# A hybrid decoder trunk on one core: first two projection units of layer 2 computed from g times the residual sum

## The reference, cut to what matters

```python
z = x @ w_in[l]            # -> q | k | v | conv h, B, C | mem q | gate_a | gate_c | gate_m
...
x = layer_norm(ALPHA * x + mix, ln1_g[l], ln1_b[l])
x = layer_norm(ALPHA * x + ffn(x), ln2_g[l], ln2_b[l])
```

## Time and profile before

| | |
|---|---|
| median of 3 runs | 1547.05 us (1546.71 to 1547.48) |
| profiled execution | 1547.15 us, span of its core 1545.4 us |
| mean granted TensorE clock | 0.996 of full speed |
| TensorE busy | 1523.5 us, 99% of the span |
| VectorE / ScalarE / GpSimd busy | 1124.1 / 928.3 / 144.8 us |
| DMA | 416.62 MB, mean 270 GB/s |

### The profile page before, as it was taken

The page is one execution under the profiler, slowest core; times in us unless marked ns, Lnnn a source line. Parts: engine busy times, 40 slices in busy tenths (PEclk is TensorE's granted clock), DMA queues, the critical chain, the costliest instruction groups (busy, mean ns, idle before and its releaser), DMA issues.

```text
span 1545.4 us, 22921 instructions
## 1 busy us (share of the span) xinstructions
PE 1523.5 (99%) x9077; PEld 1349.0 (87%) x9077; DVE 1124.1 (73%) x1043; ACT 928.3 (60%) x974; POOL 144.8 (9%) x182
## 2 busy tenths in 40 slices
PE   8999999999999999999999999999999999999997
PEld 7999999999999899999688888888888888888786
DVE  5547658844443636567798888888888888889997
ACT  5444445633333654444677777777777777767775
POOL 3203003300002103002230000000000000020000
PEclk9999999999999999999999999999999999999999
DMA  9845634694444345432799999999999999999981
GB/s 311 276 140 173 174 112 142 241 378 145 148 140 154 122 150 161 134 110 82 269 392 389 395 390 357 384 383 390 369 351 382 386 387 362 361 389 377 392 322 61
DMA packets 226425, 416.62 MB, mean 270 GB/s; under 512 B 8592, under 2 KB 110368, under 8 KB 224752
## 3 DMA queue, kind: packets, MB, share of 16 engines
q1 hardware_dynamic: 217712, 383.28, 70.4%
q0 software_dynamic: 8608, 31.89, 5.7%
HBM read 393.99 MB, written 23.11 MB: 270 GB/s over the span
## 4 chain that ended last, share of the span: by engine, by line
PE 96%; DVE 2%; ACT 1%; DMA 0%; issue 0%; POOL 0%; SPq 0%; DVEq 0%; POOLq 0%; ACTq 0%
PE ps L1950 13%; PE ps L1952 13%; PE ps L1951 13%; PE ps L2485 11%; PE ps L2487 11%; PE ps L2486 11%; PE ps L2467 5%; PE ps L2469 5%; PE ps L2468 5%; PE ps L2496 1%; PE ps L2046 1%; PE ps L2017 1%; PE ps L1985 0%; PE ps L1986 0%; PE ps L1987 0%; PE ps L2074 0%
## 5 line engine op out<-in xcount | busy, mean ns | idle before, releaser
L1338 DVE TENSOR_TENSOR low<-raw,high 128x2048 fp32r<-128x2048 f32 x264 | 603.7, 2291 | 88.0 <-ACT high L948 86.7
L948 ACT ACTIVATE high<-raw 128x2048 fp32r<-128x2048 f32 x264 | 505.9, 1919 | 197.3 <-PE ps L2487 125.1
L1348 DVE TENSOR_TENSOR low<-raw,high 128x2048 fp32r<-128x2048 f32 (+1 forms) x91 | 206.7, 2274 | 196.9 <-ACT high L941 196.8
L1950 PE MATMUL ps<-xh,high 128*128 128x320 f32 x1056 | 332.1, 315 | 4.3 <-DVE xl L1561 2.7
L1951 PE MATMUL ps<-xh,low 128*128 128x320 f32 x1056 | 327.6, 310 | 0.0
L1952 PE MATMUL ps<-xl,high 128*128 128x320 f32 x1056 | 327.6, 310 | 0.0
L2485 PE MATMUL ps<-high,xeh 128*128 128x512 f32 (+1 forms) x768 | 291.5, 380 | 0.0
L2487 PE MATMUL ps<-high,xel 128*128 128x512 f32 (+1 forms) x768 | 288.8, 376 | 0.0
L2486 PE MATMUL ps<-low,xeh 128*128 128x512 f32 (+1 forms) x768 | 287.6, 374 | 0.0
L941 ACT ACTIVATE high<-raw 128x2048 fp32r<-128x2048 f32 (+1 forms) x91 | 172.2, 1892 | 144.1 <-PE ps L1952 120.4
L1950 PEld LDWEIGHTS ps<-xh,high 128*128 128x128 f32 x1056 | 199.8, 189 | 10.8 <-issue 9.4
(11 more groups left out here) (398 smaller groups left out, 1671.9 us busy)
## 6 DMA issues: line engine op xcount, KB each, us to landing
raw<-in_exp_w_gate_dram SPq DMA_DIRECT2D x88, 1024.0 KB, 7.7
raw<-in_exp_w_up_dram SPq DMA_DIRECT2D x88, 1024.0 KB, 7.6
raw<-in_exp_w_down_dram SPq DMA_DIRECT2D x88, 1024.0 KB, 7.5
raw<-in_w_in_dram SPq DMA_DIRECT2D x37, 1024.0 KB, 5.3
ybuf<-zeros POOLq DMA_DIRECT2D x12, 1024.0 KB, 19.8
raw<-in_ffn_w_gate_dram SPq DMA_DIRECT2D x11, 1024.0 KB, 5.3
raw<-in_ffn_w_up_dram SPq DMA_DIRECT2D x11, 1024.0 KB, 6.7
raw<-in_w_o_dram SPq DMA_DIRECT2D x8, 1024.0 KB, 5.1
```

What stands on the lines that cost most here:

```text
L948: act.activation(high[(N_DENSE + m) % HI_RING][:, :], raw_moe[s][:, :], ACT.Copy).then_inc(hi_done, 1)
L1338: dve.tensor_tensor(low_moe[s][:, :], raw_moe[s][:, :], high[(N_DENSE + m) % HI_RING][:, :].bitcast(F32), ALU.subtract).then_inc(lo_done, 1)
L1348: dve.tensor_tensor(low[n % RING][:, cols], raw[n % RING][:, cols], high[n % HI_RING][:, cols].bitcast(F32), ALU.subtract).then_inc(lo_don ...
L1950: pe.matmul(out, wh, ah, start=first, stop=False)
```

## The change

The method of the first norm is brought to the second. v = g * r is split while the down projection runs, the units z 0 and z 1 of layer 2 run on v, and their four output tiles are corrected by mean and scale on VectorE (`first_projections`) into a new SBUF tile zfix; ScalarE takes the tiles from there and adds the column of b with its bias. Other than at the first norm, unit z 0 is done with all its k ahead of unit z 1, and its two corrections stand between the normalised tiles 5 and 6. v lies where kstage and the memory tiles lie, so the loads of layer 2's first keys and values go behind unit z 1. z tile 4 goes to bank 6, and the first key transposes wait for its copy. Unit z 2 is the first to read xh and xl, with a wait for each k. The two matmuls for nothing go. The waits for the blank of `ybuf` go to the third of the twelve units of the down projection.

```diff
--- before.py
+++ after.py
@@ -360,9 +362,12 @@
...
+        v_at = (mix_at + 8 * KD * T, kstage_at)
+        vh = [at(f"vh{i}", [P, KD, TV], F32R, v_at[i]) for i in range(2)]
+        vl = [at(f"vl{i}", [P, KD, TV], F32R, v_at[i] + 4 * KD * TV) for i in range(2)]
+        V_VEC = (0, 32)
+        rscale = [stats[i][:, S1, :] for i in range(2)]
+        zfix = at("zfix", [P, 4, T], F32, mix_at + 4 * KD * T)
@@ -439,7 +444,7 @@
...
+        MEAN = (ps[:, BUSY, FOLD:FOLD + T], ps[:, BUSY, FOLD:FOLD + T], ps[:, 3, 0:T])
@@ -604,7 +610,9 @@
...
-            turn = l * (len(OUTS) - len(MEM_BORROWS)) + q - (len(MEM_BORROWS) if q >= MEM_LAST[0] else 0)
+            if (l, q) == (1, 4):
+                return 6
+            turn = l * (len(OUTS) - len(MEM_BORROWS) + (q > 4)) + q - (len(MEM_BORROWS) if q >= MEM_LAST[0] else 0)
             return 3 if (l, q) == (1, 3) else turn % 3
@@ -852,6 +860,10 @@
...
+                if l == 1:
+                    pool.wait_ge(unit_done, UNIT_OF[("z", 1, 1)] + 1)
+                    load_mem_k(1, 0)
+                    load_mem_v(1, 0)
@@ -871,11 +883,6 @@
...
-                if l == 0:
-                    pool.wait_ge(tr_mm, e0 + EVENT_NO[("wink", 0, 0)] + 1)
-                    load_mem_k(1, 0)
-                    pool.wait_ge(pv_mm, j0 + 4)
-                    load_mem_v(1, 0)
@@ -1036,16 +1043,26 @@
...
-                wait_out(act, l, ("z", f))
-                src = ps[:, out_bank(l, OUT_NO[("z", f)]), 0:T]
+                if l == 1 and f < 4:
+                    act.wait_ge(zfixed, f + 1)
+                    src, bias = zfix[:, f, :], fix[:, f, 1:2]
+                else:
+                    wait_out(act, l, ("z", f))
+                    src, bias = ps[:, out_bank(l, OUT_NO[("z", f)]), 0:T], None
+                def taken(out, of, columns):
+                    if bias is None:
+                        return act.activation(out, columns, ACT.Copy)
+                    return act.activation(out, columns, ACT.Identity, bias=bias[of, :])
@@ -1096,19 +1115,19 @@
...
-                if L == 0:
-                    v_high(KD - 2)
+                if split:
+                    v_high(L, KD - 2)
                 square(L, KD - 1)
-                if L == 0:
-                    v_high(KD - 1)
+                if split:
+                    v_high(L, KD - 1)
                 act.wait_ge(var_done, L + 1)
                 act.activation(fold_dev, fold_dev, ACT.Sqrt, bias=eps[:, 0:1]).then_inc(std_done, 1)
                 act.wait_ge(mean_mm, L + 1)
                 act.activation(stats[L % 2][:, MU, :], MEAN[L], ACT.Copy).then_inc(mean_cp, 1)
-                if L == 0:
-                    hi(UNIT_OF[("fg", 0, 0)] + AHEAD)
-                    act.wait_ge(rstd_mm, 1)
-                    act.activation(by_fold(rscale), rstd, ACT.Copy, scale=float(D)).then_inc(rscale_done, 1)
+                if split:
+                    hi(UNIT_OF[("fg", 0, 0) if L == 0 else ("z", 1, 0)] + AHEAD)
+                    act.wait_ge(rstd_mm, L + 1)
+                    act.activation(by_fold(rscale[L]), rstd, ACT.Copy, scale=float(D)).then_inc(rscale_done, 1)
@@ -1120,6 +1139,9 @@
...
+                    if L == 1 and f == 5:
+                        for q in range(2):
+                            z_copy(1, q)
@@ -1127,8 +1149,11 @@
...
-                    hi(n + AHEAD)
-                    if u[0] == "z":
+                    if l == 1 and i == 0:
+                        hi(n + 1 + AHEAD)
+                    elif l == 0 or i > 1:
+                        hi(n + AHEAD)
+                    if u[0] == "z" and not (l == 1 and i == 0):
@@ -1198,7 +1223,11 @@
...
-            act.wait_ge(y_blank, 16 * ROUNDS * NE // 2)
+                    if i == 3:
+                        act.wait_ge(y_blank, 16 * ROUNDS * NE // 2)
+                        v_columns(1)
+                    v_high(1, 2 * (i // 3) - 2)
+                    v_high(1, 2 * (i // 3) - 1)
@@ -1516,19 +1545,29 @@
...
+            def first_projections(f):
+                t = zfix[:, f, :]
+                bank = out_bank(1, OUT_NO[("z", f)])
+                wait_out(dve, 1, ("z", f))
+                link(dve.tensor_copy(fix[:, f, :], ps[:, bank, T:TV]))
+                link(dve.scalar_tensor_tensor(t, stats[1][:, MU, :], fix[:, f, 0:1], ps[:, bank, 0:T], ALU.mult, ALU.add))
+                dve.tensor_tensor(t, t, rscale[1], ALU.mult).then_inc(zfixed, 1)
@@ -1568,12 +1607,15 @@
...
-                    if f == 2 and L == 0:
-                        v_low(KD - 1)
+                    if f == 2:
+                        v_low(L, KD - 1)
                     if f >= 4:
                         low_part(f - 2)
-                    if f == 5 and L == 0:
-                        lo(UNIT_OF[("fg", 0, 0)] + AHEAD)
+                    if f == 5 and L == 1:
+                        for q in range(2):
+                            first_projections(q)
+                    if f == 5:
+                        lo(UNIT_OF[("fg", 0, 0) if L == 0 else ("z", 1, 0)] + AHEAD)
@@ -1588,6 +1630,14 @@
...
+                    if l == 1 and i < 2:
+                        if i == 1:
+                            for f in (2, 3):
+                                first_projections(f)
+                            scores(l, 0)
+                            pending = 0
+                            lo(UNIT_OF[u] + AHEAD)
+                        continue
@@ -1696,9 +1746,16 @@
...
+                if i == 4:
+                    v_low_columns(1)
+                if p >= 1 and part == 1:
+                    v_low(1, 2 * p - 2)
+                    v_low(1, 2 * p - 1)
...
+                    if p == 3:
+                        v_low(1, KD - 2)
@@ -2006,6 +2063,8 @@
...
+                if l == 1 and e == EVENTS[0]:
+                    pe.wait_ge(z_cp, 38 + 5)
@@ -2134,10 +2193,13 @@
...
+                if l == 1 and q == 4:
+                    pe.wait_ge(rscale_done, 2)
+                    return
@@ -2188,8 +2250,8 @@
...
+                if L < 2:
+                    pe.wait_ge(mean_cp, L + 1)
@@ -2199,17 +2261,30 @@
...
-                for k in range(KD):
-                    pe.wait_ge(xl_done, KD + k + 1)
-                    for q in range(4):
...
-                        last = product(ps[:, out_bank(1, q), 0:T], wh[:, c], wl[:, c], xh[:, k, :], xl[:, k, :],
-                                       k == 0, k == KD - 1)
...
+                def projection(k, q):
+                    wh, wl = parts[q // 2]
+                    c = slice(256 * k + 128 * (q % 2), 256 * k + 128 * (q % 2) + 128)
+                    return product(ps[:, out_bank(1, q), 0:TV], wh[:, c], wl[:, c], vh[1][:, k, :], vl[1][:, k, :],
+                                   k == 0, k == KD - 1)
+                pe.wait_ge(resid, KD + KD - 2)
+                pe.wait_ge(v_lo, KD + 1 + 2)
+                projection(0, 1)
+                projection(0, 2)
+                last_sums(1)
+                projection(0, 0)
+                projection(0, 3)
+                for unit in range(2):
+                    for k in range(1, KD):
+                        if unit == 0:
+                            pe.wait_ge(v_lo, KD + 1 + k + 2)
+                        for m in range(2):
+                            last = projection(k, 2 * unit + m)
+                            if (unit, k, m) == (0, 1, 1):
+                                spread(1)
+                            if k == KD - 1:
+                                last.then_inc(unit_done if m else out_mm, 1)
@@ -2260,6 +2335,8 @@
...
+                            if l == 1 and i == 2 and m == 0:
+                                pe.wait_ge(xl_done, KD + k + 1)
@@ -2348,7 +2425,6 @@
...
-            layer_norm(1)
```

More of the change, by code:

```diff
@@ L330, in build_trunk @@
         kvtok = take("kvtok", [P, 2, 3, P])
+        kstage_at = place["at"]
         kstage = take("kstage", [P, 4, 2, 256])
@@ L1046, in z_copy @@
                         to, of = slice(64 * kv, 64 * kv + 64), slice(64 * a, 64 * a + 64)
-                        act.activation(qT[to, g, :], src[of, 0:NP], ACT.Copy)
-                        last = act.activation(qS[to, :, g, :], src[of, NP:T].rearrange("p (b t) -> p b t", t=TS), ACT.Copy)
+                        taken(qT[to, g, :], of, src[of, 0:NP])
+                        last = taken(qS[to, :, g, :], of, src[of, NP:T].rearrange("p (b t) -> p b t", t=TS))
                 elif 6 <= f < 8:
@@ L1055, in z_copy @@
                     act.wait_ge(zeroed, 2 * l + 2)
-                    act.activation(qmT[:, p, :], src[:, 0:NP], ACT.Copy)
+                    taken(qmT[:, p, :], slice(0, P), src[:, 0:NP])
                     for a in range(2):
                         h = slice(64 * a, 64 * a + 64)
-                        last = act.activation(qm_diag[h, p, :, (2 * p + a) * 8:(2 * p + a) * 8 + 8],
-                                              src[h, NP:T].rearrange("p (b t) -> p b t", t=8), ACT.Copy)
```

(34 more changed lines are left out.)

41 lines of the change are left out of this document (18 added, 23 removed).

## The result

| | before | after |
|---|---|---|
| median of 13 runs each, same chip | 1546.63 us (1545.4 to 1547.48) | 1550.12 us (1548.67 to 1551.26) |
| profiled execution; span | 1547.15 us; 1545.4 | 1550.54 us; 1548.8 |

The ratio of after to before is 1.0022, with a 95% interval of 1.0015 to 1.0029. So the change costs 3.4 us (2.3 to 4.5). Forecast were +1.8 us and 1548.9; the time lies inside the range, at its slow side.

What follows compares the result with a forecast made beforehand. TensorE, busy 99% of the span, was taken to bound the kernel. A paper gain of 4.4 us lost to a 4.7 us wait left +0.3; with +1.5 for the clock, +1.8 on 1547.15 gave 1548.9 us, range 1545.0 to 1550.9.

Steps and rivals of the forecast that it cites:

- TensorE up to the scores: Second norm into layer 2: sums at 506.21, scores at 524.8 instead of 528.10, 4.4 us won on paper by 532.1.
- The new pause: TensorE in z 0, before the product of k 7: 1.6 us waiting for the low half of v tile 7.
- The point of comparison: Start of layer 2's cached-key transposes on TensorE, taken as 536.46 in the kernel before.
- VectorE: Corrections of z 0 and z 1 at 1.18 us each, the last ending at 529.54; maxima of the scores to 531.0.
- ScalarE, the mis-sized term: Last corrected tile taken at 529.6 in 1.01 us; behind the Exp load, z tile 4 copied at 536.7.
- The added wait: TensorE before the key transposes waits 4.7 us for z tile 4's copy: +0.3 against 536.46.
- The key load: Layer 2's keys, issued at 523.8, land 530.0 to 533.0 under the wait; without it, up to 0.9 us.
- The clock, the second mis-sized term: Behind the long pause before the key transposes, one 1.2 GHz stretch: +1.5 us, bounds 0 and 3.0.
- Rival 3: Fourth unit: two low-clock stretches and a late z tile 4 copy, 0.3 + 3.0 + 0.5 = +3.8, 1550.9; chance 0.15.
- Rival 1: Long pause before the key transposes swallows the slow stretch, no clock loss: +0.3, 1547.4 us; chance 0.20.
- The table load: ScalarE's Exp load behind the last corrected tile: 1.28 us, to 531.9, with no added drain of about 1.38.
- Rival 4: ScalarE's function switch at the Exp load costs more than its load: +0.4 us, 1549.3; chance 0.02.

Runs made afterwards that it cites:

- experiment 6: Kernel of Experiment 1, with TensorE doing z 1's products for k 1 to 3 before z 0's product for k 7: 1544.05 us, ratio 0.9976 to the kernel before.
- Experiment 3: Changed kernel, ScalarE taking the four corrected z tiles with a plain Copy, without the bias column: 1549.11 us, ratio 1.0011 to the kernel before.
- Experiment 1: Changed kernel, z tile 4's copy moved straight behind z tile 3's, ahead of exponentials and high weights: 1543.78 us, ratio 0.9977 to the kernel before.
- experiment 7: Changed kernel, z tile 4's copy moved between job 0's exponentials and the fifth unit's high weights: 1547.92 us, ratio 1.0002 to the kernel before.
- experiment 8: Kernel before, with only layer 2's key and value loads moved to the end of z 1: 1551.84 us, ratio 1.0029 to the kernel before.
- experiment 2: Changed kernel, eight unread column sums filling TensorE's long pause before the key transposes: 1546.73 us, ratio 0.9998 to the kernel before.
- experiment 4: Kernel before, four extra unread column sums filling its 2.70 us pause before layer 2's first product: 1545.54 us, ratio 0.9989 to it.

## Why the prediction was right or wrong

Right were the sign, the mechanism and the place; the size was half of what came, +1.8 against +3.4 by the times and +3.86 in the trace. By its own steps:

- **TensorE up to the scores.** Forecast were sums at 506.21, resuming at 510.43, scores at 523.7 and the third unit at 524.8. With the 0.41 us by which this execution came sooner, each row is within 0.2. The new pause is 1.46, forecast 1.6, and experiment 6 shows that it costs nothing.
- **The point of comparison.** I took 536.46 from the chain. The timeline has the same transposes from 536.30: the chain clips a row where the one ahead still counts. That hid 0.16 us.
- **VectorE.** The corrections took 1.18 each, the last ended at 529.2 (529.54 less 0.41), the maxima at 530.5. Right.
- **ScalarE, the mis-sized term.** "The last of the four corrected tiles is taken at 529.6, 1.01 us": it took 1.53, and so did the tile ahead of it, which itself started only behind the fourth unit's high weights at 528.04. Both together make the table load 0.9 us later than forecast, and everything behind it, since from there to the end of the copy it is the 4.8 that I had. I had carried over the row of a plain copy out of PSUM to an activation that reads SBUF and adds a column: 1.53 against 1.01 us for a tile. Experiment 3 prices the larger part of the difference.
- **The added wait.** Forecast 4.7, measured 5.38; the releaser is the one named. Experiment 1 shows that it is the queue's order, with all three pieces put behind the copy, and experiment 7 with the high weights alone.
- **The key load.** "Under the wait" held here, 8.0 us from 523.85. But it was cheap only because the wait was long: experiment 8 has it as the bound in a schedule with no such wait. What I gave for a case without the wait, up to 0.9, holds for this schedule (0.2 in experiment 1). It was too little for the kernel before, where the load meets two weight loads and has TensorE wait 2.50.
- **The clock, the second mis-sized term.** Charged +1.5, measured 2.52, inside the bounds 0 and 3.0. The step that failed is "I charge one such stretch again". Rival 3 had two, and with its half microsecond of late copy it gave +3.8, the 3.86 of the trace. That the sum fits so well is luck: its clock term was 3.0 and not 2.52, since 1.4 us of the slow stretch lay inside the pause, and its late copy 0.5 and not 1.0. Rival 1 is out by experiment 2: the slow stretch began in the pause, but did not end in it.
- **The table load.** The first exponential stands 0.01 behind the load (531.09 + 1.28, 532.38). Rival 4 is out here, and so is the drain of about 1.38 us that the Trainium skill (ScalarE: Activation LUTs, What ACT_TABLE_LOAD costs) adds to every switch of the set.

Sum: 1.8 + 0.16 + about 0.85 for ScalarE + 1.02 for the clock is 3.8, the 3.86 of the trace.

## What to carry to other kernels

Before a tile is put into a resource that another step needs, read the whole queue of the engine that must empty it: here three pieces of work ahead of one copy were worth more than two units started early, and moving that copy ahead of them put it right. Price an operation by a row with the same source and operands, not by its output shape. And where a wait is to replace a wait, ask what the longer idle time does to TensorE's clock, and which loads are in time only because of it.

## What was not expected of the hardware

- The slow stretch does not follow the length of the pause alone: none behind 1.46 us, 3.4 us behind 2.70 and behind 3.60, but some 6.8 behind 3.42 (experiment 8; by the three granted clocks there, from about 511.4 to 518.2), behind 4.66 (experiment 3, from about 534.1 to 541.0) and behind 5.38. It can begin inside the pause (535.8) or behind it (512.6). One and the same pause of 1.74 to 1.75 us (L2359, in experiment 2 above) had 3.4 us of it behind it in six traces and none in four. What decides it stays open.
- Matmuls that nobody reads, put into a pause, were worth 2.5 us at their place in the changed kernel and 0.8 in the kernel before, by the traces (3.7 and 1.7 by the ratios, whose intervals are wide).
- A slow stretch can cover waits: with it gone in experiment 4, 0.5 us of them came up.
- Loads of 1 MB that shared the queues took 13.0 (weights), 10.9 (keys) and 13.4 us (values) in experiment 8; in the changed kernel the keys took 8.0, the values 10.1, and the weight loads ahead of and behind them 5.3 and 5.9.
